# Panels in plain float32 moved under the last scan steps, and the group normalisation of a two-layer block reordered

## The reference

```python
(z_s, xbc, dt_s, qkv, z_d, b_d, a_d, gate_s, gate_d) = jnp.split(u @ w_in[l], split_points, axis=-1)
y_s = mamba2_branch(z_s, xbc, dt_s, ...)      # conv, chunked scan, then:
#   yg = y * silu(z)            split in 4 groups of 512
#   yg = yg * rsqrt(mean(yg * yg, per group) + EPS) * norm_w
y_d = deltanet_branch(qkv, z_d, b_d, a_d, ...)
#   q = l2_norm(q) * 128 ** -0.5 ;  k = l2_norm(k) ; gated delta rule in chunks
merged = sigmoid(gate_s) * (y_s @ ssm_w_branch[l]) + sigmoid(gate_d) * (y_d @ dn_w_branch[l])
```

## Time and profile before

| | us |
|---|---|
| median of three runs | 2302.59 |
| range of the runs | 2299.76 to 2304.95 |
| the profiled execution, its time | 2300.63 |
| its span | 2298.7 |
| PE busy | 2154.1 (94%) |
| DVE busy | 1341.4 (58%) |
| ACT busy | 1159.0 (50%) |
| mean granted TensorE clock | 0.973 of full |

### The profile page before, as it was taken

One profiled execution on the slowest core, in us unless ns is written; L12 is line 12 of the kernel. 1 busy time (PEld: TensorE's weight loads), 2 busy tenths in 40 slices (PEclk: granted clock), 3 DMA queues, 4 the chain that ended last, 5 costly groups with the idle time before them and its releaser, 6 DMA issues. The chain is left out here.

```text
span 2298.7 us, 41083 instructions
## 1 busy us (share of the span) xinstructions
PE 2154.1 (94%) x15684; PEld 1885.5 (82%) x15684; DVE 1341.4 (58%) x1853; ACT 1159.0 (50%) x1703; POOL 61.3 (3%) x74
## 2 busy tenths in 40 slices
PE   6999889999999998988999999999999987999998
PEld 4787778878888977878998887887997886998887
DVE  3436465555557966564655555555886566556555
ACT  3454544445445566653545445445557663535444
POOL 0000000000000010000000000000011000000000
PEclk9999999999999998998999999999999998999999
DMA  9653245545553544321455554554454322254553
GB/s 401 244 229 108 83 148 189 193 165 187 193 186 130 182 145 140 119 75 57 149 183 192 193 188 167 190 192 148 165 183 129 137 86 74 74 184 183 186 193 124
DMA packets 53328, 373.24 MB, mean 162 GB/s; under 512 B 6304, under 2 KB 6304, under 8 KB 9280
## 3 DMA queue, kind: packets, MB, share of 16 engines
q1 hardware_dynamic: 47664, 342.00, 41.2%
q0 software_dynamic: 5520, 29.23, 3.6%
HBM read 370.10 MB, written 1.11 MB: 161 GB/s over the span
## 5 line engine op out<-in xcount | busy, mean ns | idle before, releaser
L1411 ACT ACTIVATE HI<-ring 128x1024 fp32r<-128x1024 f32 x614 | 633.0, 1054 | 782.1 <-PE banks L535 399.4
L1955 DVE TENSOR_TENSOR LO<-ring,HI 128x1024 fp32r<-128x1024 f32 x326 | 398.8, 1225 | 374.1 <-ACT HI L1411 368.5
L1961 DVE TENSOR_TENSOR LO<-ring,HI 128x2048 fp32r<-128x2048 f32 x139 | 318.5, 2291 | 272.8 <-ACT HI L1411 272.7
L499 PE MATMUL banks<-UH,HI 128*128 128x256 f32 x1456 | 428.0, 294 | 1.8 <-issue 1.8
L500 PE MATMUL banks<-UL,HI 128*128 128x256 f32 x1456 | 417.0, 286 | 0.0
L501 PE MATMUL banks<-UH,LO 128*128 128x256 f32 x1456 | 416.4, 286 | 0.0
L533 PE MATMUL banks<-HI,UH 128*128 128x512 f32 x896 | 350.0, 391 | 7.1 <-DVE LO L1961 4.9
L535 PE MATMUL banks<-HI,UL 128*128 128x512 f32 x896 | 349.4, 390 | 0.0
L534 PE MATMUL banks<-LO,UH 128*128 128x512 f32 x896 | 349.4, 390 | 0.0
L499 PEld LDWEIGHTS banks<-UH,HI 128*128 128x128 f32 x1456 | 284.7, 196 | 20.6 <-issue 19.8
L500 PEld LDWEIGHTS banks<-UL,HI 128*128 128x128 f32 x1456 | 284.9, 196 | 1.2 <-issue 1.2
(11 more groups left out here) (325 smaller groups left out, 3065.5 us busy)
## 6 DMA issues: line engine op xcount, KB each, us to landing
ring<-in_w_stream SPq DMA_DIRECT2D x315, 1024.0 KB, 4.8
ARENA<-in_ada_stream POOLq DMA_DIRECT2D x16, 1024.0 KB, 5.1
ARENA<-in_ada_stream SPq DMA_DIRECT2D x8, 1024.0 KB, 15.2
GRMS<-cum_rows POOLq DMA_DIRECT2D x16, 256.0 KB, 3.6
ARENA<-in_na_bias POOLq DMA_DIRECT2D x2, 1024.0 KB, 14.9
RMS<-cum_rows POOLq DMA_DIRECT2D x8, 256.0 KB, 3.4
RSTD<-cum_rows POOLq DMA_DIRECT2D x8, 256.0 KB, 3.6
ARENA<-in_ropes POOLq DMA_DIRECT2D x1, 1088.0 KB, 20.4
```

Of the source, the lines that this page charges most:

```text
L499: nc.tensor.matmul(out, lh, rh, start=start, stop=False, **kw)
L1411: nc.scalar.activation(HI[:, q % PARTS, at], ring[:, q % RING, at], ACT.Copy).then_inc(hi_ready, 1)
L1955: nc.vector.tensor_tensor(LO[:, q % PARTS, at], ring[:, q % RING, at], HI[:, q % PARTS, at].bitcast(F32), ALU.subtract).then_inc(lo_ready, 1)
L1961: nc.vector.tensor_tensor(LO[:, q % PARTS, :], ring[:, q % RING, :], HI[:, q % PARTS, :].bitcast(F32), ALU.subtract).then_inc(lo_ready, 2)
```

## The change

- PLAIN grows by panels 24 and 25, the first two z panels. Their four halves are computed by PE after scan steps 12, 13, 14 and 15 (Z_SLOTS), in float32 from the ring. ACT no longer rounds them in steps 11 and 13, DVE no longer writes their LO in steps 12 to 15. DVE gets one new wait ahead of the z stage: lo_ready for the end of panel 25.
- Each group sum has a place of its own (GROUP_AT: a bank and a column half), and one Sqrt of 128 x 1024 over banks 6 and 7 takes all four roots in place of four of 128 x 256. The q and k spreads move to banks 0 to 3.
- In the z stage PE's order within one j is now panel, qk_spread, group_sum, head_sums2. It was panel, head_sums2, group_sum, qk_spread.
- The tail is reordered: late_wide(0, 0) and head_products(0) come ahead of group_sum(3), late_wide(0, 1) behind it, and the second half of each later pair of panels moves likewise. The wait for all four roots moves from head_products(0) to head_products(1). ACT takes Silu of z for j = 7 ahead of rounding panel 33, and DVE scales q and k ahead of writing its LO.

```diff
--- before.py
+++ after.py
@@ -88,12 +88,14 @@
 LEVELS = 5
 UNITS_DN = 4 * LEVELS
 TURNS_DN = 4 + UNITS_DN
-GROUP_BANKS = (0, 0, 7, 0)
-Q_BANKS = (1, 2, 3, 6)
+GROUP_AT = ((7, 1), (6, 1), (6, 0), (7, 0))
+GROUP_SLOT = (3, 1, 0, 2)
+Q_BANKS = (0, 1, 2, 3)
 PREP_BANKS = ((0, 1, 2), (3, 6, 7))
 O_BANKS = (2, 3, 6, 7)
 SCAN_CONV = 6
-PLAIN = range(20, 24)
+PLAIN = range(20, 26)
+Z_SLOTS = {12: (24, 0), 13: (24, 1), 14: (25, 0), 15: (25, 1)}
 ROW_BUFFERS = 4
 SCAN_SLOTS = (1, 3, 6, 8, 10)
 assert len(SCAN_SLOTS) == SCAN_CONV - 1
@@ -1058,6 +1060,9 @@
                             j = L_CONV - SCAN_CONV + 1 + p
                             half = plain_half if j in PLAIN else wide_half
                             half(w0 + j, Q_LAYERS + LQ_WIDE + j, rounds, j % 2, i - at)
+                    if i in Z_SLOTS:
+                        j, e = Z_SLOTS[i]
+                        plain_half(w0 + j, Q_LAYERS + LQ_WIDE + j, rounds, j % 2, e)
 
                 def one_hot(row):
 
@@ -1080,14 +1085,13 @@
                     return mm
 
                 def group_sum(g):
-                    if g == 2:
-                        pe.wait_ge(qkrms_ready, 2 * l + 2)
-                    elif g:
-                        pe.wait_ge(yrms_ready, 4 * l + (g + 1) // 2)
+                    if g:
+                        pe.wait_ge(qkrms_ready, 2 * l + (2 if g == 3 else 1))
                     pe.wait_ge(ysq_ready, 4 * l + g + 1)
+                    b, column = GROUP_AT[g]
                     for e in range(4):
                         at = g % 2 * 1024 + e * S
-                        mm = nc.tensor.matmul(bank[GROUP_BANKS[g]][:, 0:S], MEAN_G[:, :], SQ[:, at:at + S], start=(e == 0),
+                        mm = nc.tensor.matmul(bank[b][:, column * S:column * S + S], MEAN_G[:, :], SQ[:, at:at + S], start=(e == 0),
                                               stop=(e == 3))
                     mm.then_inc(yss_done, 1)
 
@@ -1099,20 +1103,17 @@
                     spread_rows(c, QROOT[:, c // 2, :], Q_BANKS).then_inc(qkb_done, 1)
 
                 for j in range(L_ZS):
-                    wide(w0 + L_CONV + j, Q_LAYERS + LQ_WIDE + L_CONV + j, rounds, j % 2)
+                    if L_CONV + j not in PLAIN:
+                        wide(w0 + L_CONV + j, Q_LAYERS + LQ_WIDE + L_CONV + j, rounds, j % 2)
+                    if 4 <= j:
+                        qk_spread(j - 4)
+                    if j % 2 == 1 and j >= 3:
+                        group_sum((j - 3) // 2)
                     if 1 <= j <= 4:
                         mm = head_sums2(j - 1)
                         if j % 2 == 0:
                             mm.then_inc(qkss_done, 1)
-                    if j % 2 == 1 and j >= 3:
-                        group_sum((j - 3) // 2)
-                    if 4 <= j:
-                        qk_spread(j - 4)
-                group_sum(3)
-
-
-                pe.wait_ge(yrms_ready, 4 * l + 4)
-                pe.wait_ge(qk_ready, 4 * l + 4)
+
 
                 def late_wide(j, e):
 
@@ -1127,7 +1128,11 @@
 
                 def head_products(g):
 
-                    if g >= 2:
+                    if g == 0:
+                        pe.wait_ge(qk_ready, 4 * l + 4)
+                    elif g == 1:
+                        pe.wait_ge(yrms_ready, 4 * l + 4)
+                    else:
                         pe.wait_ge(v_taken, 4 * l + g - 1)
                         pe.wait_ge(weights_ready, 4 * l + g - 1)
                         pe.wait_ge(aqk_ready, 4 * l + g - 1)
@@ -1299,16 +1304,18 @@
                         mm = nc.tensor.matmul(bank[6 + b][:, at], VN[:, g, at], AQK[:, g, at], start=(t == 0), stop=True)
                     mm.then_inc(o_done, 1)
 
+                late_wide(0, 0)
                 head_products(0)
+                group_sum(3)
+                late_wide(0, 1)
                 head_products(1)
-                late_panel(0)
                 values_turn(0)
                 values_turn(1)
-                late_wide(1, 0)
+                late_panel(1)
                 head_products(2)
-                late_wide(1, 1)
+                late_wide(2, 0)
                 head_products(3)
-                late_panel(2)
+                late_wide(2, 1)
                 values_turn(2)
                 keys_turn(0)
                 values_turn(3)
@@ -1727,10 +1734,10 @@
                         if j + PARTS not in PLAIN:
                             ahead(LQ_WIDE + j)
                         conv_in(j, j % 2, True)
-                def group_rms(g):
-                    act.wait_ge(yss_done, 4 * l + g + 1)
-                    nc.scalar.activation(GRMS[:, g, :], bank[GROUP_BANKS[g]][:, 0:S], ACT.Sqrt,
-                                         bias=EPST[:, :]).then_inc(yrms_ready, 1)
+                def group_rms():
+                    act.wait_ge(yss_done, 4 * l + 4)
+                    nc.scalar.activation(GRMS[:, :, :].rearrange("p (b g) n -> p b (g n)", b=2), bank_pair[3][:, :, :], ACT.Sqrt,
+                                         bias=EPST[:, :]).then_inc(yrms_ready, 4)
 
                 def group_squares(g):
                     act.wait_ge(yg_ready, 8 * l + 2 * g + 2)
@@ -1747,8 +1754,9 @@
 
                 act.wait_ge(y_taken, 8 * l + 8)
                 for j in range(L_ZS):
-                    ahead(LQ_WIDE + L_CONV + j)
-                    act.wait_ge(panel_used, 2 * (used0 + LQ_WIDE + L_CONV + j + 1))
+                    if j < L_ZS - 1:
+                        ahead(LQ_WIDE + L_CONV + j)
+                    act.wait_ge(lo_ready if L_CONV + j in PLAIN else panel_used, 2 * (used0 + LQ_WIDE + L_CONV + j + 1))
                     if j >= 2:
                         act.wait_ge(yg_ready, 8 * l + j - 1)
                     nc.scalar.activation(tiles(ZT[:, j % 2, :], 2), tiles(bank[4 + j % 2][:, :], 2),
@@ -1764,11 +1772,10 @@
                         group_squares(j // 2 - 1)
                     if j in (3, 5):
                         qk_root((j - 3) // 2)
-                    if j in (4, 6):
-                        group_rms((j - 4) // 2)
+                split_half(Q_LAYERS + LQ_WIDE + L_CONV + L_ZS - 1 + PARTS, 0, rounds)
                 group_squares(3)
-                group_rms(2)
-                group_rms(3)
+                split_half(Q_LAYERS + LQ_WIDE + L_CONV + L_ZS - 1 + PARTS, 1, rounds)
+                group_rms()
 
                 def late_gate(j):
 
@@ -2433,19 +2440,16 @@
                         scan_out(i // 2 - 1)
                     for p, at in enumerate((-2,) + SCAN_SLOTS):
                         if 4 <= i - at <= 5:
-                            j = L_CONV - SCAN_CONV + p + PARTS
-                            if j not in PLAIN:
-                                dve.wait_ge(lo_ready, 2 * (Q_LAYERS + LQ_WIDE + L_CONV + ROUND * rounds))
-                                split_half(Q_LAYERS + LQ_WIDE + j, i - at - 4, rounds)
                             convolve_tile(L_CONV - SCAN_CONV + p, p % 2, i - at - 4)
                 scan_out(7)
 
                 def group_norm(g):
                     dve.wait_ge(yrms_ready, 4 * l + g + 1)
-                    need(step(nc.vector.reciprocal(GRMS[:, g, :], GRMS[:, g, :])))
+                    rms = GRMS[:, GROUP_SLOT[g], :]
+                    need(step(nc.vector.reciprocal(rms, rms)))
                     for e2 in range(4):
                         x_ = CONV[:, 4 * g + e2, :]
-                        ins = nc.vector.scalar_tensor_tensor(x_, x_, pk2("ssm_norm", 4 * g + e2), GRMS[:, g, :],
+                        ins = nc.vector.scalar_tensor_tensor(x_, x_, pk2("ssm_norm", 4 * g + e2), rms,
                                                              ALU.mult, ALU.mult)
                     ins.then_inc(ys_ready, 1)
 
@@ -2465,8 +2469,10 @@
                         ins = nc.vector.tensor_tensor(x_, x_, bank[Q_BANKS[g]][:, 0:S], ALU.mult)
                     ins.then_inc(qk_ready, 1)
 
+                dve.wait_ge(lo_ready, 2 * (Q_LAYERS + LQ_WIDE + PLAIN[-1] + 1 + ROUND * rounds))
                 for j in range(L_ZS):
-                    ahead(LQ_WIDE + L_CONV + j)
+                    if j < L_ZS - 1:
+                        ahead(LQ_WIDE + L_CONV + j)
                     dve.wait_ge(wide_free, 2 + WIDE0 + L_WIDE * l + L_CONV + j + 1)
                     x_ = CONV[:, 2 * j:2 * j + 2, :]
                     nc.vector.tensor_tensor(x_, x_, tiles(ZT[:, j % 2, :], 2), ALU.mult).then_inc(yg_ready, 1)
@@ -2474,6 +2480,7 @@
                         qk_reciprocal((j - 3) // 2)
                     if j >= 4:
                         qk_norm(j - 4)
+                ahead(LQ_WIDE + L_CONV + L_ZS - 1)
 
                 def late_low(j):
                     ahead(LQ_WIDE + L_CONV + L_ZS + j)

```

## The result

The changed kernel takes **2272.6 us** (median of 4 runs, 2270.8 to 2278.4), beside 2302.0 for the kernel before on the same chip: a ratio of 0.9879, 95% interval 0.9861 to 0.9897. The forecast was 2282.0 with a range down to 2276.

A forecast was written before the change was run, and what follows sets the result against it. PE, busy 2154.1 of 2298.7 us, bounds the kernel; only its idle or low-clock stretches can gain. 5.3 - 1.5 + 0.6 + 5.9 = 10.3 us per layer, 20.6 for two: median 2282 us, 8-in-10 range 2276 to 2291.

The forecast's parts named there:

- Term 1: Scan steps 12 to 15: plain halves at a 4.72 us pitch, panel 25 done at 903.2 us, no PE wait.
- Term 2: Start of the z stage: head_sums2(0) at 906.9 us, 5.3 us earlier, after a new 3.7 us idle stretch.
- Term 3: Z stage behind the new idle stretch: the clock falls once, costing 1.5 us (bounds 0 and 5.8).
- Term 4: Inside the z stage: ACT leaves out two group roots, so PE's wait ahead of qk_spread(2) goes, 0.6 us.
- term 5: Tail of z stage: waits go and group_sum(3) runs at full clock, less 0.8 us new wait at values_turn(1): 5.9 us.
- no wait for the mix: Rival, scan steps 12 to 15: ACT's exponentials set the pace and the scan stays spaced, 2289.6 us; chance 0.12.
- no new wait in the tail beyond the 0.8: Rival, z stage's tail: its gain turns into a new wait, half the 5.9 us comes back, 2288 us; chance 0.12.
- the clock down for 3.4 us and not 12.9 or longer: Rivals, z stage: clock low for the first stretch's length, 2290.6 us, chance 0.05; or through panels 26 to 31, slower, 0.02.
- the phase of later dips of the clock either way: Part of the forecast's own range, 2277 to 2287 us: later clock dips could move the time up or down, unsized.

The follow-up runs named there:

- the order alone: Changed kernel without the two plain z panels, keeping order, places of the sums and the one root: 2287.6 us, ratio 0.993 against the kernel before.
- three small edits: Stacked on the changed kernel: ACT's wait for the last y later (2268.3 us), LO of panel 26 early (2261.9), half of panel 33 between the values_turns (2259.1).

## Why the prediction was right and wrong

- **Term 1** (end of the scan): right. Pitch 4.73 us, panel 25 done at 903.39 for 903.2, no wait for the mix.
- **Term 2** (the new wait): right. Head_sums2(0) at 907.13 for 906.9, after 3.75 us that ACT's squares end. The place of the wait was right too: taking it away took the 3.7 us away.
- **Term 3** (the clock): right, one stretch of 3.4 us behind it, and its 1.5 us came back where the idle time was taken away.
- **Term 4** and **term 5**: right in sum, 6.9 us in the first layer with the order alone for 6.5. The new wait is 0.78 us for 0.8, the root 1.12 us for 1.1 and ready 2.50 us behind the sum's end for 2.4. The rule of the Trainium skill (ScalarE: Activation LUTs, section What ACT_TABLE_LOAD costs) that gives each load a drain of about 1.38 us on top would have had it ready 3.8 us behind. The trace does not agree: the load starts 0.09 us after group_sum(3) ends and the root 0.01 us after the load. PE waited 0 us for it, with 0.2 us to spare.
- The **rivals** all fell: no wait for the mix, no new wait in the tail beyond the 0.8, the clock down for 3.4 us and not 12.9 or longer.

**The step that failed** is behind the sum, where the prediction says "the phase of later dips of the clock either way": it puts the stages that the change does not touch at zero, give or take. The range's lower end of 2276 is named for no fall of the clock (3 us) and no wait at values_turn (1.6 us), so it left only 1.4 us for them. I let the change end at the inverse stage. The sum was 20.6; the two profiles differ by 28.2. Of the 7.6 us between, 2.2 lie in the changed stretches (10.6 + 12.2 - 20.6; 1.6 of it one low stretch at the start of the second scan, priced by the 155.9 against 154.3), 3.8 in the two inverse stages, and 1.6 in the rest. The rest of the 9.4 us miss, about 1.7, is mainly the profiled execution of before, which stood 2.0 us below its median, while that of after stands 0.4 below. Over four profiles each the means are nearer: 25.6 us, of which 22.8 in the scan and z stages and 3.8 in the inverse stages, less 1.1 ahead of the first scan.

So the mechanism was right and the terms, as far as the runs tell them apart, within 1 us. The size of what I had called noise was off, and I had centred it on zero. Nor was it the clock's dips alone: in the first layer's inverse stage of the first profile it was idle time that went, at a lower clock than before. The trace of the kernel before could have warned me: its scans have a low-clock stretch at the start, and in the inverse stages PE is idle for some 18 us in short pieces, at a granted clock of 0.90 to 0.92. A lower end at about 2270 would have been the right one. By how much the range was missed is partly luck: the four medians of the changed kernel, two of them with nops, are 2272.6, 2274.9, 2273.1 and 2275.8, the last only 0.2 us below 2276. That the gain is larger than 20.6 us is not luck: by the ratios it is 25 to 29 us in all four.

**What stays open** is how far this surplus is a rule. In both kernels the low stretches move between executions of one and the same program, so part is chance. Against pure chance stands the count: the stretch at the scan's start in eight of eight scans before and four of eight after; the inverse stage never below 101.5 us before and seven times of eight after. The five other kernels of the experiments, all of them shorter ahead of this stage, lean the same way: with the changed kernel's, 16 of 18 inverse stages are below 101.5 us, and 10 of 18 scans have the stretch at their start. It can't be a matter of where PE's code lies as far as 64 and 128 nops can show. I have no run that moves the start of the inverse stage and changes nothing else, so what ties its length to the stage ahead of it wasn't tried.

## What to carry to other kernels

Where the lower clock takes short stretches, a change that removes idle time is worth its waits plus what the clock gives back. Here the stages behind it became shorter as well, for a reason that stays open. So profile the kernel before two or three times, put the spread of the untouched stretches into the range, and don't take it for granted that it is centred on zero. Try the parts alone and compare stretches cut at the same instructions: here the parts added up within 0.1 us in the first layer's changed stretch, while the whole times were too coarse by some 3 us to show it. And when a wait gives place to another, look at once at the new one; three small edits behind this change were worth another 13.5 us by the medians.

## What the runs showed of the hardware

- One Sqrt over two whole banks (128 x 1024) takes 1.12 us, where 128 x 256 took 0.47: 0.85 ns per column, (1.12 - 0.47) / 768, so four small ones cost 0.76 us more than one large one, table loads aside. On DVE one subtraction of 128 x 2048 takes 2.29 us, where two halves took about 1.22 each.
- A low-clock stretch of 3.4 us costs by where it falls. In dense matmuls it was 1.5 us. At the small-product stage the same stretch, moved from just ahead to inside, lengthened the stage by 3.1 us (109.7 to 112.8), of which 0.8 was left at the next scan's start.
- The same program differs by some 6 us between executions, 2270.5 and 2276.4 us of span, with the same waits in the changed stage. The largest piece, 4.2 us between the layers, goes with one more low-clock stretch of 6.8 us.
- An inverse stage can be shorter at a lower granted clock: 99.7 us at 0.88 against 101.5 at 0.92, with 2.9 us less idle time of PE.
